# Delta-rule passes of a two-block layer: six of a pass's projection blocks move from its end to three places inside it, and the gate tile is read out of its PSUM bank five chunks sooner

## The reference, cut to what matters

```python
h = rms_norm(x, norm_g[l])
proj = jnp.matmul(h, w_in[l]).astype(jnp.float32)
q, k, v, z_att, u_shift, z_rwkv = jnp.split(proj, splits, axis=-1)
att = dilated_mixture_attention(q, k, v, pos) * jax.nn.silu(z_att)
rwk = rwkv7_time_mix(u_shift, z_rwkv, ...)
# in rwkv7_time_mix, for each of 16 heads of 64 channels, token by token:
sa = jnp.einsum('bhij,bhj->bhi', state, a_t)
state = state * w_t[:, :, None, :] + sa[..., None] * b_t[:, :, None, :] + v_t[..., None] * k_t[:, :, None, :]
y = jnp.einsum('bhij,bhj->bhi', state, r_t)
```

## Time and profile before

| | |
|---|---|
| median of 3 runs | 3251.92 us (3248.51 to 3256.41) |
| the profiled execution | 3262.28 us, its span 3260.2 us |
| TensorE matmuls busy | 3120.8 us, 96% of the span |
| GpSimd, VectorE, ScalarE busy | 50%, 41%, 35% |
| mean granted TensorE clock | 0.986 of full |

### The profile page before, as it was taken

The page is one execution under the profiler, slowest core; times in us unless marked ns, Lnnn a source line. Parts: engine busy times, 40 slices in busy tenths (PEclk is TensorE's granted clock), DMA queues, the critical chain, the costliest instruction groups (busy, mean ns, idle before and its releaser), DMA issues.

```text
span 3260.2 us, 48753 instructions
## 1 busy us (share of the span) xinstructions
PE 3120.8 (96%) x19084; PEld 2447.5 (75%) x19084; DVE 1336.1 (41%) x1974; ACT 1142.4 (35%) x1524; POOL 1638.2 (50%) x1319
## 2 busy tenths in 40 slices
PE   5999999999899999999999989999999999999997
PEld 4788888878678888888877857777777777775586
DVE  8788862110332221231231054345346346345512
ACT  4355553233432332232333243233233233244421
POOL 2565554444567777777754434443444444352242
PEclk9999999999999999999999999999999999998998
DMA  4556665332222222222222332222222222223432
GB/s 151 151 179 181 177 185 171 103 132 101 77 73 92 96 84 93 85 95 93 84 81 80 115 111 98 79 100 81 72 100 81 72 101 82 84 82 112 135 109 90
DMA packets 126966, 347.99 MB, mean 107 GB/s; under 512 B 59872, under 2 KB 62944, under 8 KB 96240
## 3 DMA queue, kind: packets, MB, share of 16 engines
q1 hardware_dynamic: 126832, 346.00, 32.4%
HBM read 306.33 MB, written 34.90 MB: 105 GB/s over the span
## 4 chain that ended last, share of the span: by engine, by line
PE 81%; issue 7%; DVE 5%; POOL 4%; ACT 2%; DMA 0%; ACTq 0%; SPq 0%; POOLq 0%; DVEq 0%
PE bank L183 23%; PE bank L185 22%; PE bank L184 22%; POOL wlo L167 4%; PE bank L1759 2%; PE bank L1087 1%; PE bank L1105 1%; PE bank L481 1%; PE bank L471 1%; PE bank L470 1%; PE bank L1441 1%; PE bank L1452 1%; DVE g L846 1%; PE bank L1760 1%; ACT whi L162 1%
## 5 line engine op out<-in xcount | busy, mean ns | idle before, releaser
L167 POOL TENSOR_TENSOR wlo<-wraw,whi 128x512 fp32r<-128x512 f32 (+1 forms) x916 | 1239.0, 1383 | 1354.2 <-ACT whi L162 1354.1
L183 PE MATMUL bank<-rhi,whi 128*128 128x512 f32 x3648 | 1482.0, 406 | 86.4 <-DVE rlo L716 28.6
L185 PE MATMUL bank<-rhi,wlo 128*128 128x512 f32 x3648 | 1429.4, 392 | 0.0
L184 PE MATMUL bank<-rlo,whi 128*128 128x512 f32 x3648 | 1428.8, 392 | 0.0
L183 PEld LDWEIGHTS bank<-rhi,whi 128*128 128x128 f32 x3648 | 688.9, 189 | 291.9 <-issue 85.0
L185 PEld LDWEIGHTS bank<-rhi,wlo 128*128 128x128 f32 x3648 | 689.0, 189 | 148.0
L184 PEld LDWEIGHTS bank<-rlo,whi 128*128 128x128 f32 x3648 | 690.0, 189 | 143.5 <-issue 11.8
L162 ACT ACTIVATE whi<-wraw 128x2048 fp32r<-128x2048 f32 (+2 forms) x232 | 437.8, 1887 | 543.1 <-PE bank L185 329.3
L915 POOL TENSOR_TENSOR wraw<-wraw,vec 128x512 f32<-128x512 f32 x260 | 267.4, 1059 | 0.0
L828 DVE TENSOR_TENSOR ssum<-ssum,wk 128x512 f32<-128x512 f32 x30 | 21.5, 718 | 314.5 <-ACT wk L818 314.5
L818 ACT ACTIVATE wk<-bank 128x512 f32<-128x512 f32 x32 | 27.9, 872 | 239.2 <-PE bank L185 239.2
(11 more groups left out here) (362 smaller groups left out, 3095.2 us busy)
## 6 DMA issues: line engine op xcount, KB each, us to landing
wraw<-in_wall_dram SPq DMA_DIRECT2D x224, 1024.0 KB, 4.9
g<-in_bmat_dram SPq DMA_DIRECT2D x16, 512.0 KB, 3.9
g<-scr_e SPq DMA_DIRECT2D x128, 64.0 KB, 3.2
scr_a<-ssum SPq DMA_DIRECT2D x24, 256.0 KB, 2.0
g<-in_xp_dram SPq DMA_DIRECT2D x4, 1024.0 KB, 12.0
g<-in_cmat_dram SPq DMA_DIRECT2D x16, 256.0 KB, 7.5
scr_u<-wk SPq DMA_DIRECT2D x16, 256.0 KB, 2.4
scr_y<-wk SPq DMA_DIRECT2D x16, 256.0 KB, 3.1
```

Source lines behind the costliest of these rows:

```text
L167: ins = pool.tensor_tensor(wlo[:, slot, c], wraw[:, slot, c], whi[:, slot, c].bitcast(F32), ALU.subtract)
L183: pe.matmul(acc[slot][:, :], whk, rhi[:, k, :], start=(k == first), stop=False)
L184: pe.matmul(acc[slot][:, :], whk, rlo[:, k, :], start=False, stop=False)
L185: ins = pe.matmul(acc[slot][:, :], wlk, rhi[:, k, :], start=False, stop=(k == last))
```

## The change

Three `fill` calls on TensorE become longer by two blocks each, or are new; the final `fill(128)` of a pass issues six fewer, since it takes what is left. On VectorE `aside(d, p, 3)` moves from behind the loop over the chunk steps (in pass 7 from its third step) to behind its first step.

```diff
                 d.scalar_tensor_tensor(nx, banks[4][:, c * CH:(c + 1) * CH], w["ex"][:, c:c + 1], nx,
                                        ALU.mult, ALU.add).then_inc(rw_sc, 1)
-                if not nxt and c == 3:
+                if c == 1:
                     aside(d, p, 3)
                 if not nxt and c >= 5:
                     xb_add(d, c - 5)
-            if nxt:
-                aside(d, p, 3)
...
             ins.then_inc(rw_tv, 1)
-            fill(5)
+            fill(7)
             pe.wait_ge(rw_sq, p + 1)
...
                 level_x().then_inc(rw_xp, 1)
-                fill(3 if nxt else 2)
+                fill((3 if nxt else 2) + (2 if l == 0 else 0))
...
             ins.then_inc(rw_gm, 1)
+            fill(2)
             for b, e, hd in quads:
                 c = 2 * b + e
                 if c < NC_ - 1:
```

## The result

The changed kernel took 3267.35 us (median of 8 runs, 3262.47 to 3269.53) against 3255.07 for the kernel before in the same comparison (8 runs, 3248.51 to 3258.08): a ratio of 1.0041, 95% interval [1.0032, 1.0051]. It is slower by 12 us, 0.4%, and the interval leaves out 1. The forecast was 3254 us, that is 2 us more than before and no measurable change, with a range of 3243 to 3266. The loss is six times the forecast one, though nearly every wait stands where the forecast put it. Between the forecast time and the measured one lie 13 us, and 3 of them are no effect of the change: over eight runs the median of the kernel before is 3255.07, where the forecast started from 3251.92.

A forecast was written before the change was run, and what follows sets the result against it. TensorE's matmuls, busy 96% of the span, were taken as the bound, so only its idle time could change. About +1 us for seven looped passes and +2 together gave 3254 us from a 3251.92 median, range 3243 to 3266.

The forecast's parts named there:

- the gap step: Idle time inside line 1516, read as an instruction page behind a weight load: 0.25 us left, inserted blocks cover nothing, shift +2.2.
- Sum of squares, second level: Lines 1403 and 1441: two more blocks at each cover waits of 0.95 and 1.05 us; shifts +0.4, then +0.7.
- Fifth level, a new wait: Behind `level_x`: tile 4 begins earlier and waits 1.5 us for VectorE's read-out of tile 2; shift +2.2.
- Chunk steps: The aside's 0.68 us hides behind the first step unless VectorE waits for SP's stores; tile 5 gives 0.3; shift +1.9.
- Mean sum, tile 7: Late in the pass: tile 6 waits 0.65 us for GpSimd, tile 7 1.6 for VectorE's read-out (2.85 without relief).
- Rivals 1 and 3: Tile 7: VectorE gets no relief, 3263 us, chance 0.17; or tile 7 does not wait, 3243 us, chance 0.12.
- rival 4: Tile 4's bank is free or the page comes without wait, and tile 6 too: down to 3244 us, chance 0.08.
- Sum: Looped pass: about 3.6 us of idle time go, 3.75 come; pass end +0.1 us, +1 us in seven passes.
- Last pass: Pass 7: 1.37 us gained ahead of 1441, variance sum 1.6 us later, +1 at the end; +2 us together.

The follow-up runs named there:

- The held loads: Fifth 1 MB weight load held on SP until the second gate product: in the kernel before 0.9959, in the changed kernel 1.0049.
- the held load: Changed kernel with the fifth weight load, and the store behind it, held on SP in passes 0 to 6: 1.0049 to the kernel before.
- The slowed chain: Kernel before with four more vector operations in VectorE's closing chain of the last pass, TensorE's blocks unmoved: 1.0024.
- the one with thinned levels: Kernel before with one block fewer at each of the last pass's five levels (1 in place of 2): 1.0034.
- the best kernel: Changed kernel with levels of 5, 2, 2, 2, 2 blocks in passes 0 to 6 and the last pass as before: 3232.60 us, 0.9926 to the kernel before.

## Why the prediction was wrong, step by step

The forecast was +2 us and the measurement +12. Two steps failed: the gap step, whose terms were short by half a microsecond seven times over, and the last pass, where the clock's part stood at nothing. The waits themselves were foreseen.

- **Sum of squares, second level.** Right: shifts of 0.37 and 0.59 in pass 2 where 0.4 and 0.7 stood.
- **Fifth level, a new wait.** Right in kind and size: 1.50, shift 2.16 against 2.2.
- **The gap inside line 1516.** The mechanism was right (its place in 1508, the load's traffic as its cause, TensorE running again at 71.79 us from the pass's start where I had 71.67), and so was the remark that the blocks behind it cover nothing. The sizes were short: 0.5 us left, not 0.25, and the two blocks take 2321.49 - 2319.90 = 1.59 us with their transitions, not 1.37. The shift was 2.7 at the first chunk step, not 2.2. I let the packet move with the load alone, by 0.7; it came 0.8 later, 69.4 us from the pass's start against 68.6. The held loads show what that left out: with no load in its way the packet moves with TensorE.
- **Chunk steps.** Right: the aside hides, tile 5 gives 0.3 back. The condition that I named (stores that are not over) is what the held load brought about.
- **Mean sum, tile 7.** Right: the waits are 0.40 and 1.59 by their brackets, with 0.1 to 0.2 for the modelled ends 0.55 and 1.75, against 0.65 and 1.6. VectorE got its relief: its first product took 1.55 us, the last two 0.69. The variance sum was 3.1 later, not 2.6, all of it carried over from above. Rivals 1 and 3 fall, and so does rival 4, since tiles 4 and 6 both wait in all seven passes.
- **Sum.** I had a pass end at +0.1; it is +0.88 in pass 2 and +0.97 in the mean. 0.5 comes from the gap step, 0.1 from the variance sum to tile 7, 0.15 behind it. +1 us for the loop was +6.8: the gap step's half a microsecond, seven times, is 3.5 of the 5.8 us between them.
- **Last pass.** This is the step that failed by more than a mis-sized term. TensorE's own delay is as I put it: the third score tile starts 1.0 us later in the changed kernel (112.75 from the pass's start against 111.77). I left out what that idle time does to the clock around it: a term at nothing, without a reason. Of the 5.5 us that the loop leaves, 1.0 is this delay; the granted clock of the changed kernel's runs, 0.9870 against 0.9881, is by estimate worth some 2.8 us (the runs of the kernel before took 3262.8 us at 0.985 and 3250.2 at 0.990 in the mean, so 2.5 us a thousandth). The change in the last pass alone, +5 us with a mean clock of 0.9869 over 11 runs, agrees with that. The other 1.7 us are within the intervals, and I can't place them.

Open: why the clock falls behind this tile in some profiles with the last pass of before and not in others. The slowed chain shows that a later tile goes with a lower mean clock; it does not show what decides a single fall. In the five of the nine profiles that fell, the clock had already been at half for 3.4 us earlier in the last pass (from 73 to 74 us of the pass, in the one with thinned levels from 83); in the four that did not, it had been at half there for 6.8 us (two) or not at all (two). So something ahead of the tile may have a part in it; no run tests it.

## What to carry to other kernels

Moving cover into a gap is worth the gap only if nothing else already covers it: here a new wait ahead of the gap had absorbed most of it, and two blocks then cost 2.35 us a pass in place of a gain. Keep the number of blocks ahead of a bank's read-out as it was, and take blocks for a new place from places that have more cover than they need (here the looped levels from the second on, which lost one block each without a listed wait), not from the pass's end, where they cover another engine. How much cover a level needs has to be tried: in the last pass, with its two blocks a level, one less cost 11 us. An idle TensorE at the start of a new phase should be priced with the clock: look at the granted clock in the profile from there on, and at the mean clock of many runs, since one profile can mislead.

## What the runs showed of the hardware

- TensorE stood 1.6 us a pass for its instructions beside a 1 MB load; issuing the load 7.7 us later (71.0 us from the pass's start, before 63.3) removed it, 11.5 us in seven passes by the periods and 13 by the ratio, with TensorE's stream unchanged.
- A load does not always hold the packet back until its traffic is over. In the best kernel it is issued at 2305.95, and the packet goes out amid its traffic (DMA view from 2308.6 to 2309.0, in slices of 0.01 us; the second queue row is the instruction packet), 65.1 us from the pass's start; with the load held it starts at 63.5. So the load delayed it by 1.6 us there, by 2.2 in the changed kernel and by 3.3 in the kernel before. What sets this length, no run here shows.

```profile
2305.95 0.35 SPq L149 DMA_DIRECT2D wraw<-in_wall_dram  x1
```

```profile
q1 hardware_dynamic: 15, 0.12, 74.6%
q8 instruction: 1, 0.02, 14.5%
```

- 1.3 us more of delay for one tile brought 8 us, with a mean granted clock of 0.9850 against 0.9881 and 23.9 us at half clock behind the tile in the profile.
- Two profiles of equal instructions show 20.5 and 6.8 us at half clock at the same place. The time of the kernel before goes with its mean granted clock, some 2.5 us for a thousandth (76 runs).
